# Neighbourhood attention with two query blocks per step, five steps a chunk, values first and scores last

## What is computed

```python
def nat_mixer(h, w_qkv, q_g, k_g, rpb, w_out):
    ...
    q = rmsnorm(qkv[:, :, 0], q_g) * (NAT_HEAD_DIM ** -0.5)
    k = rmsnorm(qkv[:, :, 1], k_g)
    v = qkv[:, :, 2]
    ...
        sc = jnp.einsum('bhqd,bhrqwd->bhqrw', q_r, k_win).astype(jnp.float32)
        sc = sc + bias.transpose(0, 2, 1, 3)[None].astype(jnp.float32)
        p = jax.nn.softmax(sc.reshape(b, NAT_HEADS, GRID_W, kh * NAT_KW), axis=-1)
        ...
        return jnp.einsum('bhqrw,bhrqwd->bhqd', p, v_win)
    ...
    return out @ w_out
```

## Time and profile before

| | before |
|---|---|
| median of 3 runs | 3220.57 us (3219.99 to 3220.60) |
| profiled execution, its own time | 3221.97 us |
| its span, first to last instruction | 3220.2 us |
| mean granted TensorE clock | 0.994 |
| TensorE matmuls busy | 3153.6 us, 98% |
| VectorE, ScalarE, GpSimd busy | 1437.1, 1256.2, 1541.7 us |
| the eight chunks' attention, from the first chunk's tokens to the last values | 1238 to 1452 us of the span |

### The profile page before, as it was taken

One profiled execution on the slowest core, in us unless ns is written; L12 is line 12 of the kernel. 1 busy time (PEld: TensorE's weight loads), 2 busy tenths in 40 slices (PEclk: granted clock), 3 DMA queues, 4 the chain that ended last, 5 costly groups with the idle time before them and its releaser, 6 DMA issues. The chain is left out here.

```text
span 3220.2 us, 34873 instructions
## 1 busy us (share of the span) xinstructions
PE 3153.6 (98%) x13869; PEld 2463.0 (76%) x13869; DVE 1437.1 (45%) x2682; ACT 1256.2 (39%) x1854; POOL 1541.7 (48%) x764
## 2 busy tenths in 40 slices
PE   8999999999999999999999999999999999899999
PEld 5668888875788887668888877787888886588887
DVE  5564111388533344445343533322534358753433
ACT  5563222245433335553343322222434345543333
POOL 3225555567354553334554534443555557545544
PEclk9999999999999999999999999999999999899999
DMA  4212323221232333222323322222332332123232
GB/s 182 76 46 92 99 92 98 92 72 52 79 99 94 96 98 102 89 79 88 103 92 98 110 74 71 74 84 67 92 100 91 97 99 66 40 92 104 92 97 87
DMA packets 80675, 286.03 MB, mean 89 GB/s; under 512 B 9089, under 2 KB 9345, under 8 KB 80385
## 3 DMA queue, kind: packets, MB, share of 16 engines
q1 hardware_dynamic: 80512, 283.80, 27.5%
HBM read 281.40 MB, written 2.10 MB: 88 GB/s over the span
## 5 line engine op out<-in xcount | busy, mean ns | idle before, releaser
L2247 POOL TENSOR_TENSOR WL<-RAW,WH 128x1024 fp32r<-128x1024 f32 x504 | 1216.8, 2416 | 1250.0 <-ACT WH L1569 1249.7
L1337 PE MATMUL PS<-XH,WH 128*128 128x512 f32 x2640 | 1072.5, 406 | 24.1 <-POOL WL L2247 22.1
L1339 PE MATMUL PS<-XH,WL 128*128 128x512 f32 x2640 | 1030.8, 390 | 0.0
L1338 PE MATMUL PS<-XL,WH 128*128 128x512 f32 x2640 | 1030.4, 390 | 0.0
L1569 ACT ACTIVATE WH<-RAW 128x1024 fp32r<-128x1024 f32 x504 | 529.0, 1050 | 539.7 <-PE PS L1339 450.6
L1337 PEld LDWEIGHTS PS<-XH,WH 128*128 128x128 f32 x2640 | 497.0, 188 | 172.6 <-issue 45.5
L1338 PEld LDWEIGHTS PS<-XL,WH 128*128 128x128 f32 x2640 | 497.1, 188 | 113.0 <-issue 16.1
L1339 PEld LDWEIGHTS PS<-XH,WL 128*128 128x128 f32 x2640 | 496.7, 188 | 105.5
L1337 PE MATMUL PS<-HH,WH 128*128 128x512 f32 x1264 | 495.7, 392 | 9.6 <-DVE HL L2145 9.6
L1338 PE MATMUL PS<-HL,WH 128*128 128x512 f32 x1264 | 493.3, 390 | 0.0
L1339 PE MATMUL PS<-HH,WL 128*128 128x512 f32 x1264 | 493.3, 390 | 0.0
(11 more groups left out here) (229 smaller groups left out, 2390.8 us busy)
## 6 DMA issues: line engine op xcount, KB each, us to landing
RAW<-wst SPq DMA_DIRECT2D x504, 512.0 KB, 3.5
BI<-natb SPq DMA_DIRECT2D x16, 384.0 KB, 4.6
X<-xin SPq DMA_DIRECT2D x16, 256.0 KB, 4.9
X<-cmpw SPq DMA_DIRECT2D x1, 2048.0 KB, 9.5
out<-X SPq DMA_DIRECT2D x8, 256.0 KB, 2.0
BI<-relm SPq DMA_DIRECT2D x4, 448.0 KB, 10.0
PRM<-prm SPq DMA_DIRECT2D x1, 685.0 KB, 12.4
BI<-rope SPq DMA_DIRECT2D x2, 256.0 KB, 3.8
```

The costliest lines, as they stand in the source:

```text
L1337: e.matmul(o, wh, h, start=first, stop=False)
L1338: e.matmul(o, wh, l, start=False, stop=False)
L1339: t = e.matmul(o, wl, h, start=False, stop=last)
L2247: e.tensor_tensor(WL[:, b % NSPLIT, :], RAW[:, b % NRAW, :], WH[:, b % NSPLIT, :].bitcast(f32), SUB).then_inc(*did(lo_made, ("lo", b)))
```

## The change

A step now handles two blocks, n and its pair (0, 1) or (2, 3). A beat runs values, turn, normalise and scores, in this order; there are five beats, due 4, 8, 12, 16 and 20 tiles after the evacuation. Both blocks' scores of one head share a PSUM bank, next to each other. VectorE begins the maxima when all four score products are there; normalise waits for the last of four exponentials. TensorE's turn and values wait for each block by itself.

```diff
-                    def scores(u):
+                    def scores(n):
+                        us = (2 * n, 2 * n + 1)
                         pair = banks.get(), banks.get()
-                        s = tiles.get()
-                        mx, nm, sm, rc = small(2), small(2), small(2), small(2)
+                        ss = tiles.get(), tiles.get()
+                        mx, nm, sm, rc = small(4), small(4), small(4), small(4)
...
-                        flight[u] = (s, sm, rc, (i, "exp", 1))
+                        flight[n] = (ss, sm, rc, (i, "exp"))
...
+                        bks, slots = (banks.get(), banks.get()), (turned.get(), turned.get())
...
                     def beat(n):
                         def f():
-                            if n < 4:
+                            if 0 <= n - 3 < 2:
+                                values(n - 3)
+                            if 0 <= n - 2 < 2:
+                                turn(n - 2)
+                            if 0 <= n - 1 < 2:
+                                normalise(n - 1)
+                            if n < 2:
                                 scores(n)
-                            if 0 <= n - 1 < 4:
-                                normalise(n - 1)
-                            if 0 <= n - 2 < 4:
-                                turn(n - 2)
-                            if 0 <= n - 3 < 4:
-                                values(n - 3)
                         return f
-                    for n in range(7):
-                        later(beat(n), 4 + 3 * n)
+                    for n in range(5):
+                        later(beat(n), 4 + 4 * n)
...
 (TensorE)
-            def nat_turn(i, s, made, slot, slot_free, bank, bank_free):
+                for n, u in enumerate(us):
+                    a = NAT_KEYS[u]
+                    for p in range(2):
+                        e.matmul(pair[p][:, NKEY * n:NKEY * n + NKEY], half(q, p)[:, 128 * u:128 * u + 128],
+                                 half(k, p)[:, a:a + NKEY], start=True, stop=True).then_inc(*did(pe_made, (i, "sc", n, p)))
+
+            def nat_turn(i, ss, i0, slots, slot_free, bks, bank_free):
                 for event in bank_free:
                     w.wait_ge(*at(event))
-                w.wait_ge(*at(made))
-                turn4(s, bank, 4, (i, "tr"))
+                for n in range(2):
+                    w.wait_ge(*at((i0, "p", n)))
+                    turn4(ss[n], bks[n], 4, (i, "tr", n))
...
 (ScalarE)
-                for p in range(2):
-                    sp = s[:, NKEY * p:NKEY * p + NKEY]
-                    w.wait_ge(*at((i, "neg")))
-                    e.activation(sp, sp, ACT.Exp, scale=1.0, bias=nm[:, p:p + 1], accum_out=sm[:, p:p + 1]).then_inc(
-                        *did(act_made, (i, "exp", p)))
+                for n in range(2):
+                    w.wait_ge(*at((i, "neg", n)))
+                    for p in range(2):
+                        sp, x = ss[n][:, NKEY * p:NKEY * p + NKEY], 2 * n + p
+                        t = e.activation(sp, sp, ACT.Exp, scale=1.0, bias=nm[:, x:x + 1], accum_out=sm[:, x:x + 1])
+                t.then_inc(*did(act_made, (i, "exp")))
...
 (VectorE)
                 for p in range(2):
                     w.wait_ge(*at(("nat_in", h + p)))
-                    w.wait_ge(*at((i, "sc", p)))
...
+                    w.wait_ge(*at((i, "sc", 1, p)))
```

More of the change, by code:

```diff
@@ L1125, in normalise @@
[L1125 to L1136, removed]
@@ L1138, in values @@
-                    def values(u):
-                        if u == 0:
+                        ss = tiles.get(), tiles.get()
+                        mx, nm, sm, rc = small(4), small(4), small(4), small(4)
+                        bias = [[BI[:, (2 * c + p) % 4, NKEY * x:NKEY * x + NKEY] for p in range(2)]
+                                for x in ((0, 1), (1, 2))[n]]
+                        i = step("nat_scores", q.ap, k.ap, (qt[0], kt[0]), us, [x.ap for x in pair],
+                                 [y for x in pair for y in x.free], [s.ap for s in ss], [y for s in ss for y in s.free],
+                                 bias, 2 * c, mx, nm, sm)
@@ new lines, in scores, with normalise, turn @@
+                        for p in range(2):
+                            pair[p].done((i, "max", 1, p))
+                        st["max"] = (i, "max", 1, 1)
+                        flight[n] = (ss, sm, rc, (i, "exp"))
+                    def normalise(n):
+                        ss, sm, rc, made = flight[n]
+                        i = step("nat_normalise", [s.ap for s in ss], sm, rc, made)
+                        flight[n] = (ss, i)
+                    def turn(n):
+                        ss, i0 = flight[n]
+                        bks, slots = (banks.get(), banks.get()), (turned.get(), turned.get())
+                        i = step("nat_turn", [s.ap for s in ss], i0, [x.ap for x in slots],
+                                 [y for x in slots for y in x.free], [x.ap for x in bks], [y for x in bks for y in x.free])
+                        for m in range(2):
+                            ss[m].done((i, "tr", m))
+                            bks[m].done((i, "pt", m))
+                        flight[n] = (slots, i)
@@ L1140, in values @@
+                    def values(n):
+                        if n == 0:
                             cur["ob"] = banks.get()
-                        slot, made = flight.pop(u)
+                        slots, i0 = flight.pop(n)
                         ob = cur["ob"]
-                        v = [[x.ap[:, 128 * n + 64 * p:128 * n + 64 * p + 64] for x, n in blocks[u]] for p in range(2)]
-                        i = step("nat_values", ob.ap, u, v, slot.ap, (made, *toks, *(ob.free if u == 0 else ())))
@@ L1145, in values @@
-                        slot.done((i, "pv"))
-                        if u < 3:
+                        v = [[[x.ap[:, 128 * y + 64 * p:128 * y + 64 * p + 64] for x, y in blocks[u]] for p in range(2)]
+                             for u in (2 * n, 2 * n + 1)]
+                        i = step("nat_values", ob.ap, 2 * n, v, [x.ap for x in slots], i0,
+                                 (*toks, *(ob.free if n == 0 else ())))
+                        for m in range(2):
+                            slots[m].done((i, "pv"))
@@ L1888, in pair_normalise, with nat_scores @@
                 t.then_inc(*did(dve_made, (i, "p")))
-            def nat_scores(i, q, k, qk_made, u, pair, pair_free, s, s_free, bias, h, mx, nm, sm):
+            def nat_scores(i, q, k, qk_made, us, pair, pair_free, ss, s_free, bias, h, mx, nm, sm):
                 for event in s_free:
@@ L1894, in nat_scores, with nat_normalise @@
                     w.wait_ge(*at(("nat_in", h + p)))
-                    w.wait_ge(*at((i, "sc", p)))
[L1896 to L1902, removed]
+                    w.wait_ge(*at((i, "sc", 1, p)))
+                for n in range(2):
+                    for p in range(2):
+                        x = 2 * n + p
+                        e.tensor_tensor_reduce(out=ss[n][:, NKEY * p:NKEY * p + NKEY],
+                                               in0=pair[p][:, NKEY * n:NKEY * n + NKEY], in1=bias[n][p], scale=1.0,
+                                               scalar=-3.0e38, op0=ADD, op1=MAX, accum_out=mx[:, x:x + 1]).then_inc(
+                            *did(dve_made, (i, "max", n, p)))
+                    w.wait_ge(*at((i, "max", n, 1)))
+                    e.tensor_scalar(nm[:, 2 * n:2 * n + 2], mx[:, 2 * n:2 * n + 2], -1.0, None, MUL).then_inc(
+                        *did(dve_made, (i, "neg", n)))
+            def nat_normalise(i, ss, sm, rc, made):
                 w.wait_ge(*at(made))
@@ L1905, in nat_normalise @@
                 w.wait_ge(*at((i, "rc")))
[L1906 to L1909, removed]
+                for n in range(2):
+                    for p in range(2):
+                        sp, x = ss[n][:, NKEY * p:NKEY * p + NKEY], 2 * n + p
+                        t = e.tensor_scalar(sp, sp, rc[:, x:x + 1], None, MUL)
+                    t.then_inc(*did(dve_made, (i, "p", n)))
             def two_squares(i, acc, acc_free, s, s_free, a, b, made):
```

34 lines of the change are left out of this document (14 added, 20 removed).

## The result

| | before | after |
|---|---|---|
| median | 3220.32 us (3219.42 to 3222.23, 6 runs) | 3208.23 us (3207.96 to 3209.43, 6 runs) |
| ratio, 95% interval | | 0.9961 (0.9950 to 0.9972) |
| profiled execution, its span | 3221.97, 3220.2 us | 3207.96, 3206.2 us |

The change saves 12.1 us where 9.3 were forecast; by the interval of the ratio it is 9 to 16 us. The two profiled executions differ by 14.0.

The account below looks back on a forecast made before the run. TensorE bounds (27.28 of 27.40 us busy a steady chunk). Stops 0.31, junctions 0.33, value runs 0.30 and a wait 0.19 save 1.13 a chunk, 1.34 in the last: 9.3 in all, so 3211.3 us, range 3209.0 to 3216.5.

Parts of the forecast that it names:

- Scores in a run: Score products on TensorE, two blocks at a stop: priced as before at 0.63 us a block, so 1.26, no gain.
- The bound for transposes: Transposes of two blocks in a run on TensorE may gain what values gain: another 0.30 us a chunk, total 11.6.
- Junctions: On TensorE, three from transposes to values go, 3 x 0.11 = 0.33 us a chunk; values to transposes cost 1.03.
- the wait of before: TensorE's 0.19 us wait ahead of values for the copy of the probabilities; to go, with copies 0.6 early.
- The last chunk: The eighth chunk, attention among the output product: same stops go, without the 0.19 wait, plus 0.40 idle: 1.34 us saved.
- Mid-step waits: Four new TensorE waits at the second block of turn and values: may each cost 0.11 us, nothing if already met.
- rival 3: Saving not there: mid-step waits and junctions at their dear price, 3.3 us saved, 3217.3; chance 0.12.
- The tie: At the next queries' head norm product on TensorE: ScalarE's square ends about when it is wanted, no slack, about 0.1.
- rival 2: The square is late behind VectorE's queue, TensorE waits at the norm product: 0.4 us a chunk, 3214.1; chance 0.13.
- the walk: Timing of one steady chunk across engines from its first score: inputs ready except one tie of about 0.1 us.
- The semaphore tail: Four score increments in a run: last score 0.06 us later by the page, 0.4 us in all; not charged.
- rival 4: GpSimd holds the third block's VectorE negation, up to 2.2 us a chunk: 6.2 us slower, 3226.8; chance 0.07.

Follow-up runs that it names:

- split scores: The changed kernel with a pair's scores in two stops one tile apart, all else in pairs: 3214.22 us, ratio 0.9975.
- doubled scores: The kernel before with each block's score products issued twice in a row into the same place: 3233.30 us, ratio 1.0035.
- the turned order: The kernel before, still seven beats of one block, with each beat running values, turn, normalise, scores: 3220.03 us, ratio 0.9994.

## Why the prediction missed its range, and where it was right

The mechanism and the sign were right; the time lies 0.8 us under the low end of the range. Predicted was 1.13 a chunk, measured 1.72 (27.40 to 25.68).

- *Scores in a run* is the mis-sized term: "I price them as before (0.63 a block ...)". Two blocks take 1.06, not 1.26, so 0.20 at each of two stops, 0.40 a chunk, 2.8 us in seven and 3.2 in eight. Two runs measured it alone: an added pair takes 0.43 by start times, and a run taken apart costs 0.39, of which 0.20 is left when the entry and the leaving are taken off. The step that failed is the pricing of a run by the length of a lone stop, although the values' row had shown that a run is cheaper. I gave a possible gain to the transposes and none to the scores.
- *The bound for transposes* (0.30 a chunk) was therefore in the wrong place. They gained 0.05 at one step and nothing at the other.
- *Junctions*: values to transposes came as forecast (1.02 for 1.03). The three junctions and the wait of before, averaged by start times over its seven chunks, were worth 0.59 a chunk where I had 0.52 from two of them.
- *Tile steps*: over the steady chunks they average 0.2287 for 0.2302 before. With some 55 a chunk this is another 0.1. Steps soon after a stop are near 0.231 and later ones near 0.227 in the trace, so longer stretches without a stop would shorten them. That this is the cause is only inferred. It isn't the number of stops alone, since the run with split scores has as many as before and averages 0.2288.
- These three, 0.40 + 0.07 + 0.1, are 0.57 of the 0.59 missing. The last chunk gave 2.1 for 1.34: the score term again, twice 0.20, and the rest not taken apart.
- *Mid-step waits* cost nothing where they are met (rival 3 falls): two blocks' values take 1.02 to 1.03 as in the earlier attention, two blocks' transposes no more than priced or 0.01 more behind values, and there is no idle time in the steady chunks.
- *The tie* held (rival 2), in part by luck: two errors of the walk nearly cancelled. The walk had the first maximum 1.83 after the first score; it was 1.34 (1316.80 to 1318.14). Its start was 1.20 from the earlier trace rows, and the trace of before has 1.19 in that chunk alone and 0.84 to 0.87 in the six others. So the square ended 0.64 earlier than walked (9.36 for 10.0), but the product came 0.45 earlier too (9.50 for 9.95), since two runs of scores were shorter, and the weights were loaded the moment the square was done. The runs with normalise behind scores show that the mechanism is real: a normalise of 1.3 us put ahead of the evacuation moves the square by 0.72 and costs 0.7 a chunk, and 4.5 to 5.2 us in all. So it is the place of normalise, and not "values first", that the order protects.
- *The semaphore tail* of the Trainium skill (page "TensorE: Matmul & The Clock Gate", section "The cost: per-tile semaphore tail") would, by the estimate of the prediction, put the last of four score products with an increment each 0.06 us later than the last of two. The runs don't bear it out. From the start of the last score product to the chunk's first maximum it is 0.59 us in the run with split scores (two increments behind the pause), in the changed kernel (four) and with four blocks (eight). It is 0.52 in the kernel before and with doubled scores (two increments), whose VectorE waits for other semaphores; what makes this 0.07 is open.
- *GpSimd's hold* (rival 4) missed the steady chunks by 0.15 us at the second normalise, and came in the last chunk, where it cost nothing. Its price depends on who waits: nothing in the seven steady chunks of the turned order (a negation of 2 us, TensorE never idle), 0.3 a chunk with four blocks in a step, up to 0.71 in a last chunk. Of the place that the rival named, a negation ahead of the square, no run has one, so the 2.2 a chunk stays untested.

## What to carry to other kernels

When an engine that is busy all the time changes from one kind of matmul to another and back, price the work between the changes by a run of the same length: the first and the last step are the dear ones. Group as much of one kind as buffers and waits allow, and stop where another engine's queue becomes the wait; a longer run of work on a helping engine is also a larger target for a hold by a third. When steps are merged, look at the queue of each helping engine for a short job that used to run in a gap and now stands ahead of something wanted.

## What the runs showed of the hardware

- The start times inside a stop of two score products (64 rows of weights, 256 columns) are 0.31 and 0.32 apart. In a stop of four they are 0.32, 0.215, 0.215 and 0.31 apart (the last number in each is up to the next tile), and four blocks' eight products take 1.92. The inner steps cost a third less; I had not expected a lone pair to consist of dear steps only.
- Transposes cost nothing to enter from a tile (a step of 0.23), where scores and values cost 0.09.
- A VectorE multiplication or negation from SBUF to SBUF that starts while GpSimd makes the low part of a weight block stands until that ends: up to 2.55 us instead of 0.17 or 0.35. It happens in the last chunk of every run here, and in every chunk with the turned order, with doubled scores and with four blocks in a step. A reciprocal that started in such a run took 0.18, as elsewhere (the run with split scores).
- Transposes to scores, a junction that in this attention only the run with the turned order has, costs 0.10 (0.52 instead of 0.42), half of what its expectation has for it. TensorE there:

```profile
1328.34 0.60 PE L1364 MATMUL PS<-CST,TT 128*128 128x128 f32 x4
1328.86 0.70 PE L1415 MATMUL PS<-TT 64*128 64x256 f32 x4
```
